# Opening of a fused decoder trunk: filler products on a zeroed tile, first transfers in pieces, constants in two transfers

## The reference

```python
proj = h @ w_in                                   # 1024 -> 3 * 1024 + 16
q, k, v, fg = jnp.split(proj, [hd, 2 * hd, 3 * hd], axis=-1)
log_f = jax.nn.log_sigmoid((fg + b_f).astype(jnp.float32))
c = jnp.cumsum(log_f, axis=1)                     # added to the logits of all heads
```

## Time and profile before

| | us |
|---|---|
| median of 3 runs | 1332.93 (1330.98 to 1333.79) |
| the profiled execution, its own time | 1333.88 |
| its span, first to last instruction | 1332.1 |
| PE busy in the span | 1296.4 (97%) |
| DVE, ACT, POOL busy | 938.3, 793.8, 225.8 |
| mean granted PE clock | 0.995 of full |

### The profile page before, as it was taken

The page is one execution under the profiler, slowest core; times in us unless marked ns, Lnnn a source line. Parts: engine busy times, 40 slices in busy tenths (PEclk is TensorE's granted clock), DMA queues, the critical chain, the costliest instruction groups (busy, mean ns, idle before and its releaser), DMA issues.

```text
span 1332.1 us, 29945 instructions
## 1 busy us (share of the span) xinstructions
PE 1296.4 (97%) x10381; PEld 1252.5 (94%) x10381; DVE 938.3 (70%) x1877; ACT 793.8 (60%) x1625; POOL 225.8 (17%) x208
## 2 busy tenths in 40 slices
PE   7999999999998999999998999999999999999997
PEld 7999999999887999999987899999999899999997
DVE  4765877765787877765678687776567667777665
ACT  4565666654565676664476667666446565766643
POOL 1000044420000034330001003433000000244300
PEclk9999999999999999999998999999999999999999
DMA  7432465556421455556442045555645334465562
GB/s 267 140 110 80 143 189 185 178 180 198 133 91 49 130 185 184 180 155 213 155 127 80 33 143 187 187 172 165 208 139 158 111 112 127 144 187 189 174 218 83
DMA packets 56723, 202.80 MB, mean 152 GB/s; under 512 B 6208, under 2 KB 8256, under 8 KB 56512
## 3 DMA queue, kind: packets, MB, share of 16 engines
q1 hardware_dynamic: 56640, 201.68, 47.4%
HBM read 200.61 MB, written 1.05 MB: 151 GB/s over the span
## 4 chain that ended last, share of the span: by engine, by line
PE 82%; DVE 7%; ACT 5%; issue 3%; DMA 1%; POOL 1%; ACTq 0%; DVEq 0%; POOLq 0%; SPq 0%
PE ps L385 23%; PE ps L389 22%; PE ps L388 22%; PE ps L535 2%; PE ps L553 2%; ACT probs L889 2%; DVE w_lo L1260 1%; PE ps L424 1%; PE ps L518 1%; PE ps L430 1%; PE ps L427 1%; ACT w_hi L839 1%; DMA raw<-in_weights 1%; POOL gated L1234 1%; DVE scores L1320 1%
## 5 line engine op out<-in xcount | busy, mean ns | idle before, releaser
L1260 DVE TENSOR_TENSOR w_lo<-raw,w_hi 128x1024 fp32r<-128x1024 f32 x377 | 461.1, 1225 | 230.3 <-ACT w_hi L839 228.9
L385 PE MATMUL ps<-h_hi,w_hi 128*128 128x272 f32 (+1 forms) x1752 | 508.6, 290 | 1.8 <-DVE q_rope L1526 1.0
L389 PE MATMUL ps<-h_hi,w_lo 128*128 128x272 f32 (+1 forms) x1752 | 505.8, 289 | 0.0
L388 PE MATMUL ps<-h_lo,w_hi 128*128 128x272 f32 (+1 forms) x1752 | 499.6, 285 | 0.0
L839 ACT ACTIVATE w_hi<-raw 128x1024 fp32r<-128x1024 f32 x377 | 395.0, 1050 | 147.7 <-PE ps L385 136.9
L385 PEld LDWEIGHTS ps<-h_hi,w_hi 128*128 128x128 f32 x1752 | 329.1, 188 | 8.4 <-issue 5.4
L388 PEld LDWEIGHTS ps<-h_lo,w_hi 128*128 128x128 f32 x1752 | 330.0, 188 | 0.3
L389 PEld LDWEIGHTS ps<-h_hi,w_lo 128*128 128x128 f32 x1752 | 328.9, 188 | 0.0
L385 PE MATMUL ps<-hid_hi,w_hi 128*128 128x272 f32 (+2 forms) x636 | 185.4, 292 | 2.2 <-DVE w_lo L1260 1.9
L388 PE MATMUL ps<-hid_lo,w_hi 128*128 128x272 f32 (+2 forms) x636 | 183.1, 288 | 0.0
L389 PE MATMUL ps<-hid_hi,w_lo 128*128 128x272 f32 (+2 forms) x636 | 183.0, 288 | 0.0
(11 more groups left out here) (184 smaller groups left out, 1727.3 us busy)
## 6 DMA issues: line engine op xcount, KB each, us to landing
raw<-in_weights SPq DMA_DIRECT2D x377, 512.0 KB, 3.7
cst<-in_consts SPq DMA_DIRECT2D x1, 1795.5 KB, 12.1
h<-in_x SPq DMA_DIRECT2D x2, 544.0 KB, 5.8
out<-h SPq DMA_DIRECT2D x8, 128.0 KB, 1.7
```

The costliest lines, as they stand in the source:

```text
L385: m = pe.matmul(b, whi, xhi, start=n == 0, stop=False)
L388: pe.matmul(b, whi, xlo, start=False, stop=False)
L389: m = pe.matmul(b, wlo, xhi, start=False, stop=n == len(tiles) - 1)
L1260: return dve.tensor_tensor(out_, a_, b_, op)
```

## The change

- PE first computes `FIRST_WARM` = 16 filler products on the zeroed tile `dec`, into bank 7, as soon as POOL has zeroed it. They have a semaphore of their own (`dec_zero`), so `INITS` falls from 8 to 7.
- SP issues weight units 0 and 1 in halves (512 columns, four blocks each) and the tokens in four parts of two chunks: first half of unit 0, two token parts, second half, two token parts, two halves of unit 1, unit 2, then the first 418 columns of the constants, unit 3, and the rest of the constants. The constants are reordered so that the identity, the gate's weights and bias, `pick` and the sinks come first.
- ACT and DVE split units 0 and 1 by halves, the first half of unit 0 before chunk 0 and the second before chunk 4. PE waits for a half before the first product that reads it.
- Waits for the constants: ACT and DVE wait at the gate's weights for the first part alone; PE waits for both parts after panel 3; POOL, DVE (step 4) and ACT (step 3) wait for the rest.

```diff
--- before.py
+++ after.py
@@ -55,7 +55,7 @@
 O_LEAD, O_LED = 2, 6
-X_PARTS = 2
+X_PARTS = 4
 ROW = 288
@@ -154,6 +154,7 @@
 WARM = 20
+FIRST_WARM = 16
 TABLES = "natural_log_exp_and_others"
@@ -163,11 +164,11 @@
     for name, width in (
-        ("ident", P), ("ones", P), ("perm_swa", P), ("perm_mla", P),
+        ("ident", P), ("gate_w", 2 * DC * 16), ("gate_b", 2), ("pick", HEADS), ("sinks", HEADS),
+        ("ones", P), ("perm_swa", P), ("perm_mla", P),
         ("mask_causal", SW), ("mask_window", SW),
         ("cos_swa", T), ("sin_swa", T), ("cos_mla", T), ("sin_mla", T),
-        ("ln", DEPTH * 2 * 2 * DC), ("conv", DEPTH * 2 * FC * 4), ("sinks", HEADS),
-        ("gate_b", 2), ("gate_w", 2 * DC * 16), ("rms_g", 5), ("pick", HEADS),
+        ("ln", DEPTH * 2 * 2 * DC), ("conv", DEPTH * 2 * FC * 4), ("rms_g", 5),
     ):
@@ -175,7 +176,8 @@
 CONST, N_CONST = const_columns()
-INITS = 8
+CONST_FIRST = CONST["sinks"][1]
+INITS = 7
@@ -240,7 +242,9 @@
         x_landed = [sem(f"x_landed{n}") for n in range(X_PARTS)]
-        const_landed, out_stored = sem("const_landed"), sem("out_stored")
+        const_landed, const_rest, out_stored = sem("const_landed"), sem("const_rest"), sem("out_stored")
+        raw_half = [sem(f"raw_half{u}") for u in range(2)]
+        half_hi, half_lo, dec_zero = sem("half_hi"), sem("half_lo"), sem("dec_zero")
         hi_ready, lo_ready, w_used = sem("hi_ready"), sem("lo_ready"), sem("w_used")
@@ -329,13 +333,24 @@
         def _(sp):
-            sp.dma_start(raw[0][:], weights[0]).then_inc(raw_landed[0], 16)
-            for n in range(X_PARTS):
-                part = slice(n * DC // X_PARTS, (n + 1) * DC // X_PARTS)
-                sp.dma_start(h[:, part], x_view[:, part]).then_inc(x_landed[n], 16)
-            for u in range(1, RING):
+            def halves(u):
+
+                for half, landed in ((0, raw_half[u]), (1, raw_landed[u])):
+                    cols = slice(half * UNIT // 2, (half + 1) * UNIT // 2)
+                    sp.dma_start(raw[u][:, cols], weights[u][:, cols]).then_inc(landed, 16)
+                    yield half
+
+            for half in halves(0):
+                for n in (2 * half, 2 * half + 1):
+                    part = slice(n * DC // X_PARTS, (n + 1) * DC // X_PARTS)
+                    sp.dma_start(h[:, part], x_view[:, part]).then_inc(x_landed[n], 16)
+            for half in halves(1):
+                pass
+            sp.dma_start(raw[2][:], weights[2]).then_inc(raw_landed[2], 16)
+            sp.dma_start(cst[:, 0:CONST_FIRST], consts[:, 0:CONST_FIRST]).then_inc(const_landed, 16)
+            for u in range(3, RING):
                 sp.dma_start(raw[u][:], weights[u]).then_inc(raw_landed[u], 16)
-            sp.dma_start(cst[:], consts).then_inc(const_landed, 16)
+            sp.dma_start(cst[:, CONST_FIRST:], consts[:, CONST_FIRST:]).then_inc(const_rest, 16)
@@ -375,8 +390,13 @@
                     if first:
-                        pe.wait_ge(lo_ready, un + 1)
+                        if isinstance(un, int) and un == 1:
+                            pe.wait_ge(half_lo, 2)
+                        else:
+                            pe.wait_ge(lo_ready, un + 1)
                         new.discard(u)
+                    if isinstance(un, int) and un == 1 and n == DC // 2:
+                        pe.wait_ge(lo_ready, 2)
                     if ready is not None and j == 0 and isinstance(i, int) and i == 0:
@@ -420,7 +440,12 @@
                                 pe.wait_ge(bank_free, p0 if s.shift else p0 + j - (BANKS - 1))
-                            pe.wait_ge(lo_ready, u0 + j + 1)
+                            if n:
+                                pe.wait_ge(lo_ready, u0 + j + 1)
+                            else:
+                                pe.wait_ge(half_lo, 1)
+                        if n == 0 and k == DC // 2:
+                            pe.wait_ge(lo_ready, 1)
                         m = pe.matmul(b, w_hi[slot][:, at_k], h_hi[:, k, t0:T], start=k == 0, stop=False)
@@ -608,6 +633,9 @@
+            pe.wait_ge(dec_zero, 1)
+            for _ in range(FIRST_WARM):
+                pe.matmul(ps[:, 7, 0:T], dec[:, 0:P], dec[:, P:P + T], start=True, stop=True)
             n_swap = [0]
@@ -624,8 +652,9 @@
                         m = i * 4 + j
-                        if m == 1 and a == 0:
+                        if m == 3 and a == 0:
                             pe.wait_ge(const_landed, 16)
+                            pe.wait_ge(const_rest, 16)
                         if m >= 3:
@@ -955,12 +984,21 @@
             act.preload_act_table_set(TABLES)
-            split_hi((0, 0, 1))
+            def split_half(u, half):
+
+                cols = slice(half * UNIT // 2, (half + 1) * UNIT // 2)
+                act.wait_ge(raw_landed[u] if half else raw_half[u], 16)
+                act.activation(w_hi[u][:, cols], raw[u][:, cols], ACT.Copy).then_inc(hi_ready if half else half_hi, 1)
+
             for k in range(DC):
+                if k % (DC // 2) == 0:
+                    split_half(0, 2 * k // DC)
                 if k % (DC // X_PARTS) == 0:
                 act.activation(h_hi[:, k, :], h[:, k, :], ACT.Copy).then_inc(norm_hi, 1)
-            for u in range(1, AHEAD):
+            for half in range(2):
+                split_half(1, half)
+            for u in range(2, AHEAD):
                 split_hi((u, u, 1))
@@ -991,6 +1029,8 @@
                         if m == 3:
+                            if a == 0:
+                                act.wait_ge(const_rest, 16)
                             gate_act_ops()
@@ -1193,7 +1233,7 @@
             own = Own(pool, pool_own)
-            pool.memset(dec[:].bitcast(F32), 0.0).then_inc(init_done, 1)
+            pool.memset(dec[:].bitcast(F32), 0.0).then_inc(dec_zero, 1)
             pool.memset(eps[:, 0:1], LN_EPS).then_inc(init_done, 1)
@@ -1208,7 +1248,7 @@
             pool.wait_ge(init_done, INITS)
-            pool.wait_ge(const_landed, 16)
+            pool.wait_ge(const_rest, 16)
             for a, kind in enumerate(KINDS):
@@ -1414,11 +1454,21 @@
-            split_lo(0, 0)
+            def split_half(u, half):
+
+                cols = slice(half * UNIT // 2, (half + 1) * UNIT // 2)
+                dve.wait_ge(hi_ready if half else half_hi, u + 1)
+                tt(w_lo[u][:, cols], raw[u][:, cols], w_hi[u][:, cols].bitcast(F32),
+                   ALU.subtract).then_inc(lo_ready if half else half_lo, 1)
+
             for k in range(DC):
+                if k % (DC // 2) == 0:
+                    split_half(0, 2 * k // DC)
                 dve.wait_ge(norm_hi, k + 1)
                 tt(h_lo[:, k, :], h[:, k, :], h_hi[:, k, :].bitcast(F32), ALU.subtract).then_inc(h_ready, 1)
-            for u in range(1, AHEAD):
+            for half in range(2):
+                split_half(1, half)
+            for u in range(2, AHEAD):
                 split_lo(u, u)
@@ -1479,7 +1529,7 @@
                             if a == 0:
-                                dve.wait_ge(const_landed, 16)
+                                dve.wait_ge(const_rest, 16)
                                 dve.wait_ge(init_done, INITS)
```

## The result

| | before | changed |
|---|---|---|
| median of 15 runs, us | 1332.93 (1330.98 to 1335.41) | 1335.30 (1333.41 to 1337.29) |
| ratio | | 1.0017, 95% interval 1.0010 to 1.0024 |
| profiled execution, its own time | 1333.88 | 1334.84 |
| span | 1332.1 | 1333.0 |

The change costs 2.4 us, 0.17%: the interval excludes no change, and the size is inside what the prediction called "within 0.2%". Predicted were 1334.6, with a range from 1331.8 to 1336.6.

The account below looks back on a forecast made before the run. PE bounds the kernel, but in the opening the gate waits for unit 4, so the 3.6 us gained become idle time. Profiled: 1333.88 + 0.3 (pieces) + 1.4 (clock) = 1335.6; median 1334.6, range 1331.8 to 1336.6.

Parts of the forecast that it names:

- within 0.2%: Whole kernel: a time within 2.7 us of no change, 75% (clock falls at the gate 60%, clock holds 15%).
- What binds: Opening: the gate waits for unit 4's late landing (17.27) and the splits behind it, so PE starts it at 20.00.
- The rival in which unit 4 doesn't bind: At the gate: its parts ready at 12 to 13, 4.2 us reach the end, 1328.7; 9%.
- Head: Opening up to panel 2: first product at 5.7, panel 2's end at 15.8, 3.6 us gained there, all becoming a gate wait.
- landing formula: Transfers on the queue: what has b MB up to its own end lands at 5.03 + (b - 0.524)/0.413.
- Filler products: PE's start: 16 products until 4.9, before the first real product at 5.7, at no cost; meant to lift the clock.
- The wait for the constants: PE's wait, moved behind panel 3: worth nothing, since constants landed at 16.0 before PE used them.
- Smaller pieces: Transfers of the opening: halves and first constants cost +0.3 us, between -0.2 and an upper end of 0.6.
- The clock at the gate: Gate and panel 3: idling 4.2 to 4.5 us drops PE to half clock, costing 1.4 us, ends 0 and 2.7.
- The sum: Profiled execution: 1333.88 + 0.3 + 1.4 = 1335.6; median forecast 1334.6.
- slower by over 0.2%: At the gate: half clock into panel 3's beginning plus DMA cost, 1336.2 with the upper ends; 16%.

Follow-up runs that it names:

- the order of the splits: Changed kernel with the split of the gate's weights moved from step 1 to step 0 on ACT and DVE: median 1329.76 us, 0.9974 of the kernel before.
- the order on the queue: Changed kernel with the rest of the constants issued behind unit 4: median 1329.83 us, 0.9980 of the kernel before.
- Holding the clock: Changed kernel with 30 more products on the zeroed tile between panel 2 and the gate: median 1333.56 us, 1.0003 of the kernel before.

## Why the prediction was right, point by point

- **What binds.** "PE's end of the opening is not set by PE" held, and two experiments remove the binding from either end (the order of the splits, the order on the queue). The rival in which unit 4 doesn't bind is excluded by the chain itself.
- **Head.** Forecast: first product 5.7, panel 2's end 15.8, gain 3.6. Measured: 5.11, 16.4, 3.0. The error is in the landing formula, which takes one rate for all. The first half of unit 0 came sooner (it was split from 3.60 on, not 4.4), and from 5 to 8 DMA moved 339 GB/s, not 413; three such us are 0.2 MB less, 0.5 us at 413 GB/s, and unit 2's split began at 10.86, not 10.3. Nothing of it reached the end, as said.
- **Filler products.** No cost was right. What I wrote of their use ("they are to lift the clock") was right of the clock and empty for the time: panels 1 and 2 end when they do with or without them.
- **The wait for the constants.** "Worth nothing" was right for this change, since the gate's wait came last; that the old wait opens once PE is early (by 1.06 us in the kernel before with fillers, by 0.32 in the one with the gate's split in step 0) was not seen.
- **Smaller pieces.** I took +0.3 with an upper end of 0.6. The pair of traces has +0.43, the means of four and six traces +0.8. This is the term of the sum that was too small. Against the same mean of 16.99, the pieces without the constants' cut gave +0.44 in one trace, and the cut without the pieces +0.17 and +0.18 in two. That makes 0.6 of the 0.8; traces with the same order of transfers differ by up to 0.6 (16.68 to 17.29), so the division stays open, and so does whether the shorter rows or the larger number of transfers cost the time. By the Trainium skill's 512 bytes for line rate ("DMA: Bandwidth & Descriptors", Specifications) this term would be 0; the traces have a delay, but no run here varies the row size alone.
- **The clock at the gate.** I took 1.4; the gate's products took 4.39 instead of 3.00, +1.39. The second trace has 4.23 (20.49 to 24.72), +1.2; the kernel without fillers has +2.4. Holding the clock gave back 1.7 in the median. That there is a fall, and a cost between the ends of 0 and 2.7, was worked out; that it comes out at 1.4 in the profiled execution is luck, as these three traces spread from 1.2 to 2.4. The rule cited from the Trainium skill, that activity releases the throttled state and idling lets it return ("TensorE: Matmul & The Clock Gate", What's actually happening), agrees with all of these traces.
- **The sum.** 0.43 + 1.39 is the shift of 1.81 at panel 3, against 1.7 forecast. With the mean DMA term it is 0.8 + 1.4 = 2.2, and the medians moved by 2.4. The forecast of 1334.6 was 0.7 low; the DMA term accounts for 0.5 of that if its mean is taken. The 16% given to "slower by over 0.2%" were not far from coming true, as the interval ends at 0.24%.

Against the kernel before, the shift at panel 3 in one trace and the difference of the medians agree to 1.3 us in all kernels. So nothing later takes back more than about that of what the opening gains or loses; a smaller effect is hidden by the scatter of single traces.

## What to carry to other kernels

Before an opening is made faster, follow the chain to the first instruction that waits for something other than the work being made faster; here it was a small split queued behind a large one, and that one behind 1.6 MB of constants nobody needed yet. Move that first: one digit changed on each of two engines was worth 5.5 us, while fillers, pieces and a second constant transfer without it cost 2.4. A gain that ends in a wait is not neutral on PE: here the idle time of 3.9 us brought the clock down, and the work behind it took 1.4 us longer.

## What the runs showed of the hardware that I had not expected

- With an idle time of 3.8 to 3.9 us at the gate the half clock came in all three traces, for 12 to 24 of the 24 gate products. It began before PE resumed at 20.4 to 20.5 in all three: the granted clock is 0.77 in 20.0 to 20.2 in the changed kernel, 0.82 in 19.5 to 20.0 in its second trace, and 0.63 in 19.0 to 19.5 without fillers, each time followed by 0.50. The cost does not follow from the length of the gap alone: 1.4, 1.2 and 2.4 us for 3.86, 3.75 and 3.92.
- Products on a zeroed tile raise the clock and hold it: the pace went from 0.23 to 0.13 us at 6.5 in the changed kernel, 5.3 us after the first filler, as against 8.7 in the same kernel without fillers, and 30 of them kept 1.00 over the gap.
- The first transfers are not served at the steady rate: a first transfer half as large was ready for its split 1.46 us earlier (3.60 against 5.06), which for its 0.262 MB is 180 GB/s, against 413 later. The second half, issued behind two token parts, was split from 6.72 on, later than the whole unit before.
